# Weaving the first even output chunks into the end of the first attention, and reordering the products of the memory value pieces

## What is computed

```python
y_a = a_b * conv_out                       # 512 channels
y_b = _dsa(q, qi, wi, q_pos, k_all, ...)   # 512 channels
x = x + jnp.concatenate([y_a, y_b], axis=-1) @ p["w_out_even"][e]
```

```python
hm = _rmsnorm(mem, g)
k = _rmsnorm((hm @ w_k).reshape(bsz, m, X_HEADS, X_HEAD_DIM), k_norm)
v = (hm @ w_v).reshape(bsz, m, X_HEADS, X_HEAD_DIM)
```

## Time and profile before

| what | us |
|---|---|
| median of 3 runs | 1569.79 |
| lowest and highest | 1568.76, 1569.88 |
| the profiled execution | 1568.68 |
| its span, first to last instruction | 1566.9 |
| TensorE busy | 1551.6 (99%) |
| VectorE busy | 988.8 (63%) |
| GpSimd busy | 666.2 (43%) |
| ScalarE busy | 641.0 (41%) |

### The profile page before, as it was taken

How to read it: one execution, slowest core, us unless ns; L and a number is a source line. 1 busy time by engine, 2 the same in 40 slices (tenths; PEclk the granted TensorE clock), 3 DMA queues, 4 the chain that set the end, 5 groups by cost and what they waited for, 6 DMA issues and landing times.

```text
span 1566.9 us, 30883 instructions
## 1 busy us (share of the span) xinstructions
PE 1551.6 (99%) x11966; PEld 1489.9 (95%) x11966; DVE 988.8 (63%) x1408; ACT 641.0 (41%) x953; POOL 666.2 (43%) x317
## 2 busy tenths in 40 slices
PE   9999999999999999999999999999999999999999
PEld 8889848998999999999999998999899999999999
DVE  7798895776565564555657879757657552055530
ACT  6332464546443332333335675445543332133321
POOL 4345521461343433343435757554143334343442
PEclk9999999999999999999999999999999999999999
DMA  5343321340322232222223333334122223222222
GB/s 207 133 145 100 129 82 41 108 151 26 121 81 94 80 111 77 81 80 94 96 81 104 105 102 121 105 112 148 38 84 84 91 89 105 66 90 90 89 93 95
DMA packets 42393, 153.89 MB, mean 98 GB/s; under 512 B 5632, under 2 KB 6656, under 8 KB 41032
## 3 DMA queue, kind: packets, MB, share of 16 engines
q1 hardware_dynamic: 42312, 152.75, 28.9%
HBM read 145.53 MB, written 9.30 MB: 99 GB/s over the span
## 4 chain that ended last, share of the span: by engine, by line
PE 85%; DVE 6%; issue 3%; POOL 2%; ACT 2%; DMA 0%; POOLq 0%; SPq 0%; DVEq 0%; ACTq 0%
PE PS L1087 76%; PE AX L1087 3%; POOL WLO L508 2%; DVE TB L2086 1%; DVE SC L1689 1%; ACT PX L843 1%; PE AX L1438 1%; DVE LG L1850 1%; PE AX L1320 1%; DVE RB L2088 1%; DVE SC L1672 0%; PE PS L1333 0%; DVE M L1671 0%; PE AX L1353 0%; PE AX L1142 0%
## 5 line engine op out<-in xcount | busy, mean ns | idle before, releaser
L508 POOL TENSOR_TENSOR WLO<-WRAW,WHI 128x1024 fp32r<-128x1024 f32 (+3 forms) x301 | 635.7, 2121 | 883.8 <-ACT WHI L572 883.6
L572 ACT ACTIVATE WHI<-WRAW 128x1024 fp32r<-128x1024 f32 (+3 forms) x301 | 268.7, 913 | 580.8 <-PE PS L1087 549.6
L1087 PE MATMUL PS<-XH,WHI 128*128 128x272 f32 (+1 forms) x2128 | 443.7, 290 | 0.3 <-DVE XL L1629 0.3
L1087 PE MATMUL PS<-XH,WLO 128*128 128x272 f32 (+1 forms) x2128 | 440.0, 288 | 0.0
L1087 PE MATMUL PS<-XL,WHI 128*128 128x272 f32 (+1 forms) x2128 | 437.7, 287 | 0.0
L1087 PEld LDWEIGHTS PS<-XH,WHI 128*128 128x128 f32 x2128 | 337.2, 188 | 7.8 <-issue 3.7
L1087 PEld LDWEIGHTS PS<-XL,WHI 128*128 128x128 f32 x2128 | 337.1, 188 | 0.0
L1087 PEld LDWEIGHTS PS<-XH,WLO 128*128 128x128 f32 x2128 | 335.2, 188 | 0.0
L1087 PE MATMUL PS<-HH,WHI 128*128 128x272 f32 x1216 | 252.5, 289 | 0.1
L1087 PE MATMUL PS<-HH,WLO 128*128 128x272 f32 x1216 | 251.2, 288 | 0.0
L1087 PE MATMUL PS<-HL,WHI 128*128 128x272 f32 x1216 | 251.2, 288 | 0.0
(11 more groups left out here) (322 smaller groups left out, 1852.5 us busy)
## 6 DMA issues: line engine op xcount, KB each, us to landing
WRAW<-in_w_in_even SPq DMA_DIRECT2D x29, 512.0 KB, 3.3
WRAW<-in_w_up0a SPq DMA_DIRECT2D x22, 512.0 KB, 3.2
WRAW<-in_w_up0b SPq DMA_DIRECT2D x22, 512.0 KB, 3.2
WRAW<-in_w_up1a SPq DMA_DIRECT2D x22, 512.0 KB, 3.2
WRAW<-in_w_up1b SPq DMA_DIRECT2D x22, 512.0 KB, 3.2
WRAW<-in_w_mv SPq DMA_DIRECT2D x16, 512.0 KB, 3.3
WRAW<-in_w_xq SPq DMA_DIRECT2D x16, 512.0 KB, 3.3
WRAW<-in_w_xo SPq DMA_DIRECT2D x16, 512.0 KB, 3.3
```

The source lines that it names most:

```text
L508: pool.tensor_tensor(WLO[parity][:, first:last], WRAW[parity][:, first:last], WHIf[parity][:, first:last], ALU.subtract).then_inc(lo_done, ...
L572: act.activation(WHI[parity][:, first:last], WRAW[parity][:, first:last], ACT.Copy).then_inc(hi_done, 2 // len(cuts))
L1087: ins = pe.matmul(dst, w, x, start=first, stop=last)
```

## The change

In the memory value pieces, both layers: TensorE waits for the high part of the weights only, issues the two products that need no weight remainder for both token tiles (4 matmuls), then waits for the remainder and issues the last 2.

At the end of the first attention: k-tile 0 of output chunk 0 is issued behind the scores of the last pair (turn 16), k-tile 1 ahead of the transposes of turn 17, k-tile 2 ahead of those of turn 18. Behind attention come k-tile 3 of chunk 0, k-tiles 0 to 3 of chunk 1, k-tiles 4 to 7 of chunk 0 (with its completion signal), k-tiles 4 to 7 of chunk 1, `memory_mean(0)`, and chunks 2 to 7 as before.

```diff
-                pe.wait_ge(lo_done, c * 2 + kk + 1)
+                pe.wait_ge(hi_done, c * 2 + kk + 1)
                 w = slice(512 * kk, 512 * kk + 512)
                 for mb in range(2):
                     tok, out = slice(P * mb, P * mb + P), AX[:, 2 + mb, :]
                     pe.matmul(out, MH[l][:, k, tok], WHI[c % 2][:, w], start=k == 0, stop=False)
-                    pe.matmul(out, MH[l][:, k, tok], WLO[c % 2][:, w], start=False, stop=False)
-                    ins = pe.matmul(out, ML[l][:, k, tok], WHI[c % 2][:, w], start=False, stop=k == KT - 1)
+                    pe.matmul(out, ML[l][:, k, tok], WHI[c % 2][:, w], start=False, stop=False)
+                pe.wait_ge(lo_done, c * 2 + kk + 1)
+                for mb in range(2):
+                    ins = pe.matmul(AX[:, 2 + mb, :], MH[l][:, k, P * mb:P * mb + P], WLO[c % 2][:, w],
+                                    start=False, stop=k == KT - 1)
...
+            def mixed_part(m, first, last):
+
+                c, t = C0["out_even"] + m, T0["out_even"] + m
+                if first == 0:
+                    pe.wait_ge(lo_done, c * 2 + 2)
+                    pe.wait_ge(lg_ready, len(UNITS) - 2 + 2 * m)
+                    pe.wait_ge(yl_even, A_TILES)
+                if last > A_TILES:
+                    pe.wait_ge(yl_even, A_TILES + 5)
+                for k in range(first, last):
+                    w = slice(P * k, P * k + P)
+                    cut = [slice(0, H), slice(H, T)]
+                    ins = product([PS[:, t % 2, i, 0:H] for i in range(2)], WHI[c % 2][:, w], WLO[c % 2][:, w],
+                                  [HH[:, k, c_] for c_ in cut], [HL[:, k, c_] for c_ in cut], k == 0, k == KT - 1)
+                if last == KT:
+                    ins.then_inc(chunk_done, 1)
+
             for p in range(PAIRS + 3):
+                if p in (PAIRS, PAIRS + 1):
+                    mixed_part(0, p - PAIRS + 1, p - PAIRS + 2)
...
+                if p == PAIRS - 1:
+                    mixed_part(0, 0, 1)
...
-            for m in range(LEN["out_even"]):
-                chunk(c0 + m, (c0 + m) % 2, t0 + m, (t0 + m) % 2, KT, HH, HL, yl_even if m == 0 else None,
-                      [A_TILES] * 4 + [A_TILES + 5] * 4)
+            mixed_part(0, 3, 4)
+            mixed_part(1, 0, 4)
+            mixed_part(0, 4, 8)
+            mixed_part(1, 4, 8)
+            memory_mean(0)
+            for m in range(2, LEN["out_even"]):
+                chunk(c0 + m, (c0 + m) % 2, t0 + m, (t0 + m) % 2, KT, HH, HL)
```

## The result

| kernel | median us | runs | ratio to before, 95% interval |
|---|---|---|---|
| before | 1568.64 | 8 | |
| changed | 1573.22 | 8 | 1.0028 (1.0019 to 1.0037) |
| changed, a later comparison (e15) | 1572.47 (before 1568.72) | 11 | 1.0024 (1.0015 to 1.0033) |

The change costs 3.8 to 4.6 us by the medians. The prediction said 1572.8 in a range of 1569.8 to 1575.9. The profiled execution of the changed kernel took 1572.14 us and has a span of 1570.3, 3.4 more than before. The 1569.79 us from which the prediction counted was the median of the first three of the 8 runs of before; with all 8 it is 1568.64.

The account below looks back on a forecast made before the run. TensorE, busy 99% of the span, was taken as the bound. Moved k-tiles -2.25, attention +0.5, wait at the memory mean +4.8 and layer 1 0 gave about +3.0 on 1569.79: 1572.8 us, range 1569.8 to 1575.9.

Parts of the forecast that it names:

- Attention, +0.5: End of first attention: three k-tiles moved into TensorE's gaps delay attention's last products by 0.5 us (bounds 0 to 2.35).
- B: Moment when output chunk 0 is complete, behind attention: forecast at 255.1, 1.25 us later than before (253.84).
- the 3.0 us to the mean: After B, TensorE has only 4 k-tiles of chunk 1, 3.0 us, left until the first memory mean.
- The collision: Before the first memory mean: GpSimd's chunk 3 remainder takes SBUF ahead of KSA; mean 3.0 us late, TensorE idle 4.8.
- The clock: Rival: the idle time at the first memory mean lowers TensorE's clock, costing 1.5 to 3.1 us more; chance 0.25.
- The value pieces: Layer 1: waits of 0.58 and 0.56 us at values 5 and 7 turn into next-chunk waits; gain 0, bound 1.6.
- Absorption: Behind the first memory mean, chunks 2 to 7 and later: nothing found that wins the delay back.
- KSA did not pass: Rival, first memory mean: KSA would pass ahead of GpSimd, mean 0.8 us late, time 1570.6; chance 0.12.
- Layer 1 gave nothing back: Rival: earlier values 5 and 7 let ScalarE and GpSimd go on sooner, returning up to 1.6 us; chance 0.10.
- the last case, a weave that keeps its gain: Rival: the first memory mean does not hold TensorE, 1.75 us stay won, time 1568.0; chance 0.08.

Follow-up runs that it names:

- e15: The changed kernel measured once more without any edit: 1572.47 us (before 1568.72), ratio 1.0024.
- e4: Changed kernel plus five unused matmuls issued ahead of the first memory mean, filling its idle time: 1570.96 us, ratio 1.0018.
- e1: Kernel before with only the value pieces' new product order, no k-tiles moved into attention: 1567.98 us, ratio 1.0002.
- e3: Changed kernel with VectorE adding head 0's squared key halves ahead of its sum of squares: 1567.69 us, ratio 0.9994.
- e7: Changed kernel with only k-tiles 0 and 1 of chunk 1 ahead of chunk 0's last four, means unmoved: 1566.81 us, ratio 0.9991.
- e6: Changed kernel with each memory mean one chunk later and only two chunk 1 k-tiles before chunk 0's last four: 1566.05 us, ratio 0.9982.
- e8: Changed kernel keeping the three k-tiles among the turns, but finishing chunk 0 before all of chunk 1: 1566.84 us, ratio 0.9987.
- e5: Changed kernel with each memory mean one output chunk later: 1568.01 us (before 1568.96), ratio 0.9997.
- e2: Changed kernel with the value pieces put back as before, only the k-tile moves kept: 1573.07 us, ratio 1.0030.

## Why the prediction was right, and where it was not

**The end came out close, in part by luck; the mechanism is right but for the clock.** 1572.8 was forecast; 1573.22 and 1572.47 were measured. The forecast was +3.0 from a base of 1569.79. Measured, the base is 1568.64 and the change +4.6 by the medians, +4.1 by the rows. A base 1.15 too high made up for most of what the change was put too low.

**Attention, +0.5: mis-sized, 0.** From the last scores (237.21) to attention's last products it is 5.66 us in the changed profile, and 5.66 before (243.57 - 237.91). The sum took the two groups of 8 transposes by the lengths of their rows, 1.25 and 1.2. But matmul rows overlap, and the cost is the distance between two starts: the k-tiles behind these groups start 1.01 and 0.87 behind them (239.79 - 238.78, 241.50 - 240.63). That is the 0.5, less than 0.1 on balance for the k-tiles (0.84 each and not 0.8) and the last group (0.53 and not 0.6).

**B and the 3.0 us to the mean: right.** Chunk 0 is complete 1.25 later, the forecast said; 0.8 of it came, since attention's 0.5 did not: attention's last products to VectorE's addition to X are 11.34 now (254.21 - 242.87) and were 10.54 (254.11 - 243.57).

**The collision: right, by its place and its price.** The issue of the remainder was put 0.1 behind the sum of squares; it was 0.12. KSA was to end at B + 7.75; taking B as 0.27 ahead of VectorE's addition (253.84 and 254.11 before), it ended at 261.50 - 253.94 = 7.56. The idle time was forecast at 4.8, and was 4.4. The mean is 2.42 late where 3.0 was said, 0.5 of the difference being attention's.

**The clock: ranked wrongly.** The forecast let it stay at 2.4 GHz and gave its fall 0.25. It fell, in all three profiles that have the idle time. Its price, 1.5 to 3.1, was 1.7 and 2.6. The price was taken from the first eight matmuls, 0.84 us each, though the profile lists a granted clock of 1.00 for them too (1.49 to 8.23); that they are slow all the same is seen in e4, where rows of the same shape take 0.45 each at a granted clock of 1.00. Within the change, attention's and the mean's 0.6 too much cancelled a part of the clock's 1.7 too little. By the case as it happened the sum is 2.4 + 1.7 = 4.1: 1573.9 from the base of the prediction, 1572.7 from the measured one. The step that failed is "against it: no row has a fall in it": the longest gap of before was 1.73 us, and it could say nothing about one of 4.8. The section of the Trainium skill that was cited there (page "TensorE: Matmul & The Clock Gate", "HAM oscillation — how this bites in real kernels"), by which long idle gaps of TensorE bring the clock down, was the better guide. The traces agree with it: idle times of 4.4 to 4.5 us were followed by a granted clock of 0.50 to 0.52, and in e4, the same wait filled with matmuls, it stays at 1.00.

**The value pieces: right**, 0 (e1). The waits turned into waits of the next chunk, 0.99 and 0.97 where 0.58 and 0.56 stood at the pieces, and the starts behind them are as far apart as before.

**Absorption: right.** The shift of 3.40 at chunk 2 is 3.38 in layer 1, and 3.4 at the end. Counted from attention's last products to the end of the span, it is 4.1 (1570.3 - 242.87 against 1566.9 - 243.57): 2.42 of waiting and 1.68 of clock, with nothing left over.

**The rivals.** KSA did not pass. Where it does (e3, e7), the mean is 0.4 to 1.3 earlier than before and not 0.8 later; but these are not the case of the rival. Attention's 0 takes off 0.5, and the rest is the edit's own: e3 also takes the sum of squares out of KSA's way, e7 finishes chunk 0 two k-tiles earlier. Layer 1 gave nothing back. And the last case, a weave that keeps its gain, exists as e6 and e8.

## What to carry to other kernels

Filling gaps of a full engine is worth only what its next wait leaves over: work that is interleaved finishes together, so count what the first piece's completion starts, and how much of the second is left to cover it. Where two engines hold each other up, as GpSimd and VectorE did here (KSA 2.55 us in place of 0.41), look who is issued in the middle of whose chain: swapping two short additions (e3) was worth some 5 us here. Ask of every new idle time whether it is longer than any that the old profile has; beyond that the old profile's clock is no evidence.

## What the runs showed of the hardware that I had not expected

The clock fell within attention too, in three of the twelve profiles (e5, e8, e15), in the stretch of light TensorE work around an idle time near 212 us. That idle time was 1.73 us in these three; it was 1.73 in before, e1 and e2 as well, where the clock stayed, and 1.0 to 1.43 in the six others, where it stayed too. Two of these stretches, of e5 and of e8:

```profile
213.70:217.10 3.40, 3.40 (x12) 1.24 (x9) 2.27 (x8) 1.52 (x6) 0.77 (x1) 0.50 0.42 151
```

```profile
212.90:219.60 6.70, 6.21 (x18) 2.35 (x18) 5.02 (x20) 3.40 (x11) 1.83 (x1) 0.50 0.25 78
```

These executions were among the longer ones of their kernels (1569.66, 1569.24 and 1575.14 us, where the medians are 1568.01, 1566.84 and 1572.47). The two profiles of the kernel before show no fall. But of its 35 executions beside e5 to e8, 24 have a mean granted clock of 1.000 and take 1568.2 us on average, and 11 have 0.999 or 0.998 and take 1570.3; of the 15 beside e15, 10 take 1568.8 and 5 take 1569.5. So its clock very probably falls too in some executions, and that goes with a good part of the spread of 1567.03 to 1571.27; where it falls there was not seen.

In these traces GpSimd's remainders and VectorE's additions of two tiles in SBUF take turns by whole instructions. A waiting GpSimd operation goes ahead of the next VectorE operation even when that one is issued without a pause: KSA, issued 0.63 behind the sum of squares in the change, e2 and e4, took 2.55 or 2.56 us each time, in place of 0.41.
